# A four-layer decoder step: the 64-token tile on two halves of the lanes, diagonal weights by VectorE, and first loads in another order

## What is computed

```
h = x
for i in 0..3:
    h = h + 0.5 * rmsnorm(swiglu(rmsnorm(h, g[0]), w_in[i,0], w_down[i,0]), g[1])   # 1024 -> 2 x 2816 -> 1024
    h = h + rmsnorm(mixer_i(rmsnorm(h, g[2])), g[3])
    h = h + 0.5 * rmsnorm(swiglu(rmsnorm(h, g[4]), w_in[i,1], w_down[i,1]), g[5])
```

## Time and profile before

| | us |
|---|---|
| median of 3 runs | 4714.99 (4714.24 to 4820.31) |
| the profiled execution | 4714.75 |
| its span, first to last instruction, slowest core | 4713.2 |
| spans of the eight cores | 4700.4 to 4713.2 |
| granted TensorE clock, mean of the cores | 0.994 to 0.995 |
| PE busy (30510 matmuls) | 4614.4, 98% |
| DVE, ACT, POOL busy | 1767.7, 1290.4, 644.5 |
| read from HBM | 682.92 MB |

### The profile page before, as it was taken

How to read it: one execution, slowest core, us unless ns; L and a number is a source line. 1 busy time by engine, 2 the same in 40 slices (tenths; PEclk the granted TensorE clock), 3 DMA queues, 4 the chain that set the end, 5 groups by cost and what they waited for, 6 DMA issues and landing times.

```text
span 4713.2 us, 83008 instructions; the slowest of 8 cores (4700.4 to 4713.2 us)
## 1 busy us (share of the span) xinstructions
PE 4614.4 (98%) x30510; PEld 2719.1 (58%) x30510; DVE 1767.7 (38%) x3074; ACT 1290.4 (27%) x2496; POOL 644.5 (14%) x1110
## 2 busy tenths in 40 slices
PE   7998999999999999999999989999999999999999
PEld 4555656556555555565646466565665655656564
DVE  3257232364232452326232374222633226232522
ACT  2125222233121431215121243122332225121421
POOL 2121110011010120102010211010110102010210
PEclk9999999999999999999999999999999999999999
DMA  8335636264353453534556246263642626435371
GB/s 171 60 69 113 117 67 118 50 108 84 61 105 66 89 97 62 114 63 80 101 127 111 54 79 121 54 117 57 115 83 55 122 50 123 81 72 104 54 123 41
DMA packets 228859, 416.67 MB, mean 88 GB/s; under 512 B 115103, under 2 KB 137887, under 8 KB 228446
## 3 DMA queue, kind: packets, MB, share of 16 engines
q0 software_dynamic: 88592, 319.79, 39.1%
q1 hardware_dynamic: 139870, 91.56, 8.2%
HBM read 682.92 MB, written 12.71 MB: 148 GB/s over the span
## 4 chain that ended last, share of the span: by engine, by line
PE 93%; DVE 2%; issue 1%; DMA 1%; SPq 1%; ACT 1%; POOL 0%; DVEq 0%; ACTq 0%; POOLq 0%
PE ps L83 92%; DVE big L88 1%; PE ps L84 1%; SPq L242 1%; ACT big L85 1%; DVE big L86 1%; DMA big<-xp 1%; DMA big<-wmx 1%; DVE big L89 1%; DVE big L87 0%; DMA big<-big 0%; POOL big L86 0%; DVEq L167 0%; POOL big L90 0%; POOL big L242 0%
## 5 line engine op out<-in xcount | busy, mean ns | idle before, releaser
L83 PE MATMUL ps<-big 128*128 128x384 bf16 (+6 forms) x29758 | 4581.3, 322 | 49.1 <-DVE big L86 15.0
L83 PEld LDWEIGHTS ps<-big 128*128 128x128 bf16 (+1 forms) x29758 | 2675.6, 99 | 1922.3 <-issue 139.2
L85 ACT ACTIVATE big<-ps 128x384 f32<-128x384 f32 (+4 forms) x1525 | 879.9, 580 | 2913.9 <-PE ps L83 2780.3
L86 DVE TENSOR_TENSOR big<-ps,big 128x384 bf16<-128x384 f32 (+7 forms) x1374 | 856.1, 623 | 1869.2 <-PE ps L83 1852.2
L88 DVE SCALAR_TENSOR_TENSOR big<-big 128x1024 bf16<-128x1024 f32 (+8 forms) x555 | 595.6, 1078 | 192.5 <-POOL big L86 128.5
L242 POOL DMA_DIRECT2D big<-wst x608 | 326.7, 540 | 2493.4 <-PE ps L83 2313.4
L86 POOL TENSOR_TENSOR big<-big 128x1 f32<-128x1 f32 (+1 forms) x442 | 298.2, 676 | 1518.6 <-DVE big L87 1346.8
L85 ACT ACTIVATE big<-big 128x1024 bf16<-128x1024 f32 (+5 forms) x452 | 348.2, 786 | 452.2 <-DVE big L88 312.3
L87 DVE TENSOR_SCALAR big<-big 128x1 f32<-128x1 f32 (+4 forms) x463 | 84.8, 184 | 749.3 <-ACT big L85 736.3
L84 PE MATMUL ps<-big 128*128 128x128 bf16 (+1 forms) x752 | 56.4, 219 | 40.0 <-DVE big L88 31.9
L89 DVE COPY big<-big 32x1136 bf16<-32x1136 bf16 (+2 forms) x229 | 82.8, 361 | 13.0 <-PE ps L83 4.3
(11 more groups left out here) (9 smaller groups left out, 21.1 us busy)
## 6 DMA issues: line engine op xcount, KB each, us to landing
big<-wst POOLq DMA_DIRECT2D x608, 512.0 KB, 7.7
big<-gains SPq DMA_DIRECT2D x52, 512.0 KB, 11.2
big<-xp SPq DMA_DIRECT2D x16, 512.0 KB, 9.7
yp<-big SPq DMA_DIRECT2D x16, 512.0 KB, 4.0
big<-big SPq DMA_DIRECT2D x64, 71.0 KB, 2.5
big<-big SPq DMA_DIRECT2D x64, 70.8 KB, 2.6
big<-big SPq DMA_DIRECT2D x48, 64.0 KB, 2.4
big<-dwx SPq DMA_DIRECT2D x4, 512.0 KB, 4.4
```

The source lines that it names most:

```text
L83: 'matmul': lambda e, *a, **k: e.matmul(*a, **k),
L85: 'activation': lambda e, *a, **k: e.activation(*a, **k),
L86: 'tensor_tensor': lambda e, *a, **k: e.tensor_tensor(*a, **k),
```

## The change

A tile has `split` when P is 64. Its residual then lies as channels 0 to 511 on partitions 0 to 63 and channels 512 to 1023 on partitions 64 to 127 (`parts`), 512 elements wide (`w`). The down and output projections write the two halves to partitions 0 to 63 and 64 to 127 of one PSUM bank, in place of two banks. `rstd` adds the two half sums with two partition-shifted copies. Operations with a gain are done once for each half, the others once at half the width. Transposes are 4 of 128 x 128, always on PE for this tile. Mixer 2's own v code is not touched.

`mkw` gives its product to VectorE. `chain_first` loads tokens 0, the gain row, tokens 1 and 2; weights 0 and 1 wait (on POOL) for tile 1, tokens 3 to 5 (on SP) for weight 0, weights 2 and 3 for tile 4, tokens 6 to 8 for weight 2, weights 4 to 6 for tile 7, and the rest follow. `setup` starts at planned time 105 and gets 6 us of slack after its loads. Some numbers of the planner's model change.

```diff
@@ Prog.dma
-            shared = self.dfree['pool'] > start + 1.0
-            d = max(start + 1.2, self.dfree[q]) + mb / (0.1 if shared else 0.2)
-            if shared:
-                self.dfree['pool'] += mb / 0.2
+            d = max(start + 1.2, self.dfree[q])
+            m1 = min(mb, max(0.0, 0.1 * (self.dfree['pool'] - d)))
+            d += m1 / 0.1 + (mb - m1) / 0.2
+            self.dfree['pool'] += m1 / 0.2
@@ Tok
+        self.split = P == 64
+        self.lanes = 128
+        self.w = 512 if self.split else 1024
+        self.parts = [(slice(0, 64), slice(0, 512)), (slice(64, 128), slice(512, 1024))] if self.split else [(slice(0, 128), slice(0, 1024))]
@@ w_pump
-        def w_pump():
+        def w_pump(reads=()):
...
-                    p.dma('pool', [(A.at(slot_off(k), [SLOT_EL], BF16), wst[arg])], ('w', s), writes=[('ws', s)], mb=1.0)
+                    p.dma('pool', [(A.at(slot_off(k), [SLOT_EL], BF16), wst[arg])], ('w', s), reads=reads, writes=[('ws', s)], mb=1.0)
@@ rstd, wide
+        def rstd(t, a, half=False):
+            sc = stt[:, a:a + 1]
+            if t.split:
+                o = scol()
+                p.op('dve', I.tensor_copy(out=stt[0:64, o:o + 1], in_=stt[64:128, a:a + 1]), reads=[('ss', a)], writes=[('ss', o)])
+                p.op('dve', I.tensor_copy(out=stt[64:128, o:o + 1], in_=stt[0:64, a:a + 1]), reads=[('ss', a)], writes=[('ss', o)])
+                p.op('dve', I.scalar_tensor_tensor(out=sc, in0=sc, scalar=4.0 * EPS if half else EPS, in1=stt[:, o:o + 1], op0=ALU.add, op1=ALU.add),
+                     reads=[('ss', a), ('ss', o)], writes=[('ss', a)])
...
+        def wide(t, out, in0, a, gp, gpid, reads, writes):
+
+            for ln, cs in t.parts:
+                tok = p.op('dve', I.scalar_tensor_tensor(out=out[ln, 0:t.w], in0=in0[ln, 0:t.w], scalar=stt[ln, a:a + 1],
+                                                         in1=gp[ln, cs], op0=ALU.mult, op1=ALU.mult),
+                           reads=reads + [('ss', a), gpid], writes=writes)
+            return tok
@@ post
-            tok = p.op('dve', I.tensor_tensor(out=tmp[k][0:P, :], in0=ps[0:P, :], in1=gp[0:P, :], op=ALU.mult),
-                       reads=pids + [gpid], writes=[('tmp', k)])
-            BKS.give(b, b + 1)
+            for ln, cs in t.parts:
+                tok = p.op('dve', I.tensor_tensor(out=tmp[k][ln, 0:t.w], in0=ps[ln, :], in1=gp[ln, cs], op=ALU.mult),
+                           reads=pids + [gpid], writes=[('tmp', k)])
+            pair_give(t, b)
@@ pre
-            if via == 'dma' and p.dfree['pool'] < S.now + LIGHT:
+            if via == 'dma' and not t.split and p.dfree['pool'] < S.now + LIGHT:
...
-                fns = [I.transpose(bb[:, c * 128:c * 128 + P], xmb[k][0:P, c * 128:(c + 1) * 128], identb[0:P, 0:P])
-                       for c in range(8)]
+                fns = [I.transpose(bb[:, c * 128:(c + 1) * 128], xmb[k][:, c * 128:(c + 1) * 128], identb) for c in range(nc_)]
@@ chain_first
+        FIRST = {1: (0, 2), 4: (2, 4), 7: (4, 7)}
+
+        def chain_first(g_, t):
+            reads = ()
+            if t.idx in (3, 6):
+                key = ('slot', (g_, 'fi', 0, 0, t.idx // 3 - 1, 0))
+                yield Flag(key)
+                reads = [slot_of(key[1])]
+            elif t.idx:
+                yield Flag(('xl', t.idx - 1))
+            tok = load_x(g_, t, reads)
+            if t.idx == 0:
+                load_gain(gpre, 'gpre', 0)
             S.set(('xl', t.idx))
-            if hook is not None:
-                hook()
             yield p.t(tok)
+            if t.idx in FIRST:
+                WS.cap = FIRST[t.idx][1]
+                w_pump([('h', t.idx)])
+                if t.idx == 7:
+                    WS.cap = 10 ** 9
+                    w_pump()
             yield from pre(t, gpre, 'gpre', 0, 'pe')
@@ tok_mm
-                        ps, pids = bk2(b if bb is None else bb)
+                        ps, pids = pair(t, b if bb is None else bb)
...
-                                fns.append(I.matmul(ps[0:P, hf * 512:(hf + 1) * 512], lhsT=lhs(kc, t),
+                                out = ps[64 * hf:64 * hf + 64, :] if t.split else ps[:, hf * 512:(hf + 1) * 512]
+                                fns.append(I.matmul(out, lhsT=lhs(kc, t),
                                                     rhs=wv[:, k2, hf * 512:(hf + 1) * 512], start=(kc == 0), stop=(kc == nk - 1)))
-                        return p.op('pe', fns, reads=lids(kb, t) + [wid], writes=pids)
+                        return p.op('pe', fns, reads=lids(kb, t) + [wid], writes=pids, cost=0.44 if t.split else None)
@@ mixer_a
-                yield p.rt_r(['exts_st'])
+                yield p.rt_r(['exts_st']) + 8.0
...
-                    tok = p.op('pool', I.tensor_tensor(out=wv[i], in0=sstack.unsqueeze(1).broadcast_to([128, 64, 32]),
+                    tok = p.op('dve', I.tensor_tensor(out=wv[i], in0=sstack.unsqueeze(1).broadcast_to([128, 64, 32]),
@@ setup
-            tok = p.dma('sp', [(tmp[k], wmx[:, :, :].rearrange("p a b -> p (a b)"))], 'wmx', writes=[('tmp', k)])
-            yield p.t(tok)
+            tok = p.dma('sp', [(tmp[k], wmx[:, :, :].rearrange("p a b -> p (a b)"))], 'wmx', writes=[('tmp', k)], mb=0.5)
+            yield p.t(tok) + 6.0
...
+                p.op('dve', I.tensor_copy(out=Bn[64:128, g4, :], in_=Bn[0:64, g4, :]), reads=['Bs'], writes=['Bs'])
@@ the end of build_program
-        load_gain(gpre, 'gpre', 0)
-        hooks = {0: cap(2), 2: cap(4), 4: cap(6), 6: cap(9), 8: cap(10 ** 9)}
         for t in taus:
-            S.spawn(chain_first(0, t, ('xl', t.idx - 1) if t.idx else None, hooks.get(t.idx)))
-        S.spawn(setup(), 60.0)
+            S.spawn(chain_first(0, t))
+        S.spawn(setup(), 105.0)
```

More of the change, by code:

```diff
@@ L739, in build_program @@
             slot = {}
-            cap = 2
+            cap = 0
         def slot_off(k):
@@ L804, in scol @@
             return k
[L806 to L810, removed]
+        def rstd(t, a, half=False):
[6 more added lines that the diff above has]
+                     reads=[('ss', a), ('ss', o)], writes=[('ss', a)])
+            else:
+                p.op('dve', I.tensor_scalar(out=sc, in0=sc, scalar1=EPS, scalar2=4.0 if half else 1.0, op0=ALU.add, op1=ALU.mult),
+                     reads=[('ss', a)], writes=[('ss', a)])
+            return p.op('pool', I.tensor_tensor(out=sc, in0=sc, in1=nhalf[:, 0:1], op=ALU.pow),
@@ L811, in rstd, with square @@
                         reads=[('ss', a), 'nh'], writes=[('ss', a)])
-        def square(P, src, rd):
+        def square(t, src, rd, half=False):
             a = scol()
-            tok = p.op('act', I.activation(out=junk[0:P, :], in_=src, func=AF.Square, scale=1.0 / 32.0,
-                                           accum_out=stt[0:P, a:a + 1]),
+            tok = p.op('act', I.activation(out=junk[:, 0:t.w], in_=src, func=AF.Square, scale=1.0 / 16.0 if t.split and half else 1.0 / 32.0,
+                                           accum_out=stt[:, a:a + 1]),
@@ L849, in fin @@
                     yield p.t(tok)
-                    out_toks.append(p.dma('sp', [(final, tmp[k][0:P, :])], ('st', k), reads=[('tmp', k)], mb=0.5))
+                    out_toks.append(p.dma('sp', [(final[:, cs] if t.split else final, tmp[k][ln, 0:t.w]) for ln, cs in t.parts], ('st', k), reads=[('tmp', k)], mb=0.5))
                     P_TMP.give(k)
@@ L1748, in chain_d @@
             yield p.t(tok)
-            a, tok = square(P, h[0:P, t.idx, :], [('h', t.idx)])
+            a, tok = square(t, h[:, t.idx, 0:W], [('h', t.idx)])
             yield p.t(tok)
-            tr = rstd(P, a)
+            tr = rstd(t, a)
             yield p.t(tr)
@@ L1758, in chain_d @@
             xid = ('tmp', kk)
[L1759 to L1761 removed]
+            tok = wide(t, x32, h[:, t.idx, :], a, gpre, 'gpre', [('h', t.idx)], [xid])
             S.set(('ch', k, t.idx))
@@ L1796, in fn @@
                     cs = slice(c * 128, (c + 1) * 128)
-                    if t.idx == 8:
-                        fns.append(I.matmul(dp[:, c * 128:c * 128 + 64], lhsT=hi[0:64, cs], rhs=Bn[0:64, g4, :], start=True, stop=False))
-                        fns.append(I.matmul(dp[:, c * 128:c * 128 + 64], lhsT=lo[0:64, cs], rhs=Bn[0:64, g4, :], start=False, stop=True))
+                    if t.split:
+                        ln, ch = t.parts[c // 4][0], slice((c % 4) * 128, (c % 4) * 128 + 128)
+                        fns.append(I.matmul(dp[:, c * 128:c * 128 + 64], lhsT=hi[ln, ch], rhs=Bn[ln, g4, :], start=True, stop=False))
+                        fns.append(I.matmul(dp[:, c * 128:c * 128 + 64], lhsT=lo[ln, ch], rhs=Bn[ln, g4, :], start=False, stop=True))
                     elif first:
@@ L1826, in fn2 @@
             def fn2(b):
-                mp, mpids = bk2(b)
+                mp, mpids = pair(t, b)
                 fns = []
                 for g4 in range(4):
```

(5 more changed lines are left out.)

79 lines of the change are left out of this document (40 added, 39 removed).

## The result

The changed kernel takes 4658.09 us in the median of its runs, against 4718.9 us for the kernel before in the runs of the same series. Two of the six runs of each kernel were slow ones; they count in these two medians, and are left out of all that follows. The ratio of the other runs is 0.9874, with a 95% interval from 0.9857 to 0.9891: 1.3% faster, inside the stated range, 12 us above the forecast of 4646. Its profiled execution took 4654.91 us, 59.8 less than the one before.

What follows compares the result with a forecast made beforehand. PE was taken to bound the kernel, busy 4614.4 of 4713.2 us. Split tile 41.8, start 12 and diagonals 14.5 sum to 68.3 us saved from 4714.75: forecast 4646 us, range 4628 to 4680.

Steps and rivals of the forecast that it cites:

- The split tile: 64-token tile 8 on two column halves: 400 matmuls from 85.3 to 45.7 us, plus transposes; 41.8 us saved.
- weight loads in the open: Rival for tile 8: weight loads lose their cover, its matmuls save only 20.7 us; time 4665; chance 0.08.
- no overlap: Rival for tile 8: the two column halves do not overlap at all; time 4686; chance 0.02.
- a drained array: Rival for tile 8: switching halves waits until the array is empty, 380 ns per matmul; time 4755; chance 0.03.
- The transposes: Tile 8: 88 transposes of 64 x 64 become 44 of full size, 4.6 to 2.4 us; 2.2 saved.
- shortened cover at the transitions: Stage transitions: tile 8's shorter down projection covers tile 7's chain less; costed at nothing, up to 30 us without cover.
- The diagonals: Convolution mixers of both groups: VectorE builds diagonal weights instead of POOL; two thirds of 21.9 us, 14.5 saved, bounds 5 and 20.
- PE idle there under 3 us a place: Expected sign near 300 and 2700 us, once VectorE instructions of 5 to 8 us are gone from there.
- The hold-up of POOL: VectorE's diagonal products may hold up a power on POOL by up to 2.4 us each; sum some 4 us less.
- The start: Kernel start with gated token and weight loads: PE loss from 37.3 to some 25.5 us; 12 saved, bounds 20 and minus 8.
- The wmx load moves behind 105 us: Step for the start: transfer engines are no longer full there, so PE's 7.5 us idle behind VectorE's wmx cast goes.
- The 3% rival that is slower: Tile 8: a switch of column half waits until the array is empty; time 4755, slower than before; chance 0.03.

Runs made afterwards that it cites:

- the planner experiment: Changed kernel with the planner reckoning tile 8's blocks at 0.86 us instead of 0.44: core median 4676.1 us, against 4649.4 for the changed kernel.

## Why the prediction held, and where its terms were off

**Bound by PE:** right. Busy time fell 47.7 us, and only 12.1 of the 59.8 us are idle time.

**The split tile, forecast 41.8 us, measured 43.3 alone.** The mechanism was right; that the size is so near has some luck in it, for errors cancel. The 400 matmuls had covered 90.7 us (94.1 less 3.4), not the 85.3 of the sum, and cover 46.3 now: 44.4 less, where 39.6 was forecast. By the starts a pair takes 0.216 us and not 0.2285; the 0.015 us taken from the convolution's quarters is not there. The rivals on it are refuted: weight loads in the open would give 65 us covered, no overlap 85, a drained array over 110. The transposes saved nothing, against 2.2 forecast: 716 full-size ones cover 57.5 us now. Before, 664 full-size ones covered 51.9, and the small ones 4.6, so it is 1 us more; there are 52 more full-size ones, not 44. Of the shortened cover at the transitions, priced at nothing with up to 30 us as the dear end, some 7 us came true (5.5 to 12.9 us idle), and the planner experiment shows the dear end for real: 26.7 us. These are new waits of PE in the rest of group 0, one of the signs named for a wrong forecast; they were too small to move the time out of the range.

**The diagonals, forecast 14.5, measured 14.6.** The size was right by luck, for the division was not. I took two thirds of 11.9 us in group 0 and of 10.0 in group 1; it was nothing in group 0 and 14.8 us in group 1, more than the whole loss that I had counted there. The step that failed is "PE idle there under 3 us a place" for group 0. The stall is gone, but a wait of 6.6 to 8.9 us for the prompt's shifted copies has come, and the stretch takes as long as with the stall. An idle of 9.4 us with a clear cause was taken for time that its removal gives back. The hold-up of POOL that the prediction allowed for shows once: at 2653.1 us a product of POOL that takes 0.55 us as a rule took 2.26, while a diagonal block ran on VectorE from 2652.65 for 2.28 us.

**The start, forecast 12 us, is the mis-sized term.** It is 7.3 alone and 2.9 on top of the split. By the run with the old loads the gates together have no part in it; what remains is the constants' move with the planner's new numbers, which were not tried alone. This is as much as the 8.5 us by which the sum (68.3) exceeded the profiled difference (59.8). Four steps of its working can be read in the changed kernel's timeline:

```profile
5.92 1.28 ACT L85 ACT_TABLE_LOAD   x1 [5.92 <-DMA big<-xp]
...
9.93 1.28 DVE L88 SCALAR_TENSOR_TENSOR big<-big 128x1024 bf16<-128x1024 f32 x1 [1.32 <-DMA big<-gains]
...
11.95 1.23 POOL L242 DMA_DIRECT2D big<-wst  x2 [2.64 <-DMA big<-xp]
...
21.69 2.72 PE L83 MATMUL ps<-big 128*128 128x384 bf16 x8 [1.26 <-ACT big L85]
...
37.38 11.94 PE L83 MATMUL ps<-big 128*128 128x384 bf16 x64
...
46.71 6.38 POOL L242 DMA_DIRECT2D big<-wst  x12
```

The first token landed at 5.9 (5.5 forecast), but the next loads did not follow at 2.0 us: the gain row held VectorE until 9.9, and tile 1 came at 11.4 instead of 9.5. The first four loads landed at 5.8, 9.7, 11.4 and 12.6 us: the second took 3.9 us behind the first and not the 2.0 taken from a crowded stretch. So the first FFN matmul came at 21.7, not 18. The bubble before nt1 and the burst of 12 weight issues on POOL (6.4 us, 6.6 forecast) were as worked out; nt1 came at 37 instead of 31. PE's idle in the first 100 us, 24.4, is what was forecast as "near 24", but by luck: from a start later than forecast and fewer bubbles after it.

The other step: "The wmx load moves behind 105 us". It did not. It is issued at 59.6 us and takes 23.5 us to land, nearly as before (58.5 and 24.9). The planned time moves an instruction only against its neighbours on its own queue, and SP had nothing else to do. What moved is the cast on VectorE, which now stands behind products that are due earlier, and so PE's wait of 7.5 us is gone all the same.

**The 3% rival that is slower** needed a mean spacing of 0.280 us; it was 0.108 by the starts (0.116 by the cover).

## What to carry to other kernels

A tile with half the columns costs TensorE half the time if its output can be cut in two, one part for each half of the array's columns, and a matmul for the other half is never more than four places away. In a kernel whose engine orders are planned ahead, the plan's price must follow at once; here the same matmuls with a stale price gave back 26.7 of some 43 us. A stall with a clear cause is worth what its stretch loses without it, not its length: undo one edit at a time, and time the same matmuls in both kernels stretch by stretch, before adding up gains. Before idle time is read from a profile, its matmuls should be counted against its weight loads: here 170 missing records would have made some 4 us of idle time out of nothing. And a wait for "a transfer" says nothing until the shape of the instruction that waits has told which transfer it is.

## What the runs showed of the hardware

- Overlap of matmuls on two column halves does not need strict alternation. With 64 stationary and 512 moving columns, a pair takes 0.216 us, as a single matmul did. Runs of 1, 2 and 4 on one half cover the same 49.7 us; with runs of 8 or 22 exactly four matmuls at a change of half overlap, some 0.9 us won for each change.
- Weight loads of 64 columns keep their 110 ns but overlap: 440 cover 24.1 us when halves alternate, 45.3 when they do not. The Trainium skill (TensorEngine Tiling (Array Packing), Key Properties) says that tiles load weights and multiply in parallel; these rows agree.
- In the first 13 us, with the first weight load issued at 11.95, a token tile, the gain row and two more token tiles (512 KB each, issued from 1.1 to 2.4 us) landed at 5.8, 9.7, 11.4 and 12.6 us.
- VectorE's scaling of tile 8 took 8.0 us for two halves of 512 elements while POOL built diagonal blocks, and 1.61 us when POOL did not.
